# RWKV layer: the receptance products placed right behind the keys', and the weight lows of both made on GpSimd

## The reference

```python
h = rms_norm(x, mix_norm[l])
h_prev = jnp.pad(h, ((0, 0), (1, 0), (0, 0)))[:, :-1]
dx = h_prev - h
r, k, v = jnp.einsum('sbtc,scd->sbtd', h[None] + dx[None] * mu[:3, None, None, :], w_rkv)
xw, xa, xg = h + dx * mu[3], h + dx * mu[4], h + dx * mu[5]
w_log = -softplus(-(w0 + tanh(xw @ w1) @ w2)) - 0.5
decay = exp(-exp(w_log))
a = sigmoid(a0 + (xa @ a1) @ a2)
g = sigmoid(xg @ g1) @ g2
kk = (k * k_k) by head;  kk = kk * rsqrt(max(sum(kk * kk), 1e-24))
k = k * (1 + (a - 1) * k_a)
y = wkv7_scan(r, decay, k, v, -kk, kk * a)      # then a head norm, a bonus from r * k, times g, times w_o
```

## Time and profile before

| | |
|---|---|
| median of 3 runs | 2046.4 us (2046.1 to 2047.64) |
| profiled execution: time, span | 2049.06 us, 2047.7 us |
| TensorE busy | 1993.0 us, 97% |
| VectorE busy | 1512.7 us, 74% |
| ScalarE busy | 1087.5 us, 53% |
| GpSimd busy | 164.7 us, 8% |
| weight lows on VectorE | 608, mean 1241 ns |
| weight lows on GpSimd | 34, mean 2506 ns |

### The profile page before, as it was taken

The page is one execution under the profiler, slowest core; times in us unless marked ns, Lnnn a source line. Parts: engine busy times, 40 slices in busy tenths (PEclk is TensorE's granted clock), DMA queues, the critical chain, the costliest instruction groups (busy, mean ns, idle before and its releaser), DMA issues.

```text
span 2047.7 us, 33781 instructions
## 1 busy us (share of the span) xinstructions
PE 1993.0 (97%) x13456; PEld 1808.1 (88%) x13456; DVE 1512.7 (74%) x2548; ACT 1087.5 (53%) x1661; POOL 164.7 (8%) x92
## 2 busy tenths in 40 slices
PE   8999899999999999899999999999999999999999
PEld 7997789889888998689989789989999999888888
DVE  6776784877667775877757877899899996555555
ACT  6654643266555664666645765545544445555554
POOL 0000013300011000210001013232000000000000
PEclk9999998999999999999999999999999999999999
DMA  6666231156655666246666335546544446666664
GB/s 210 202 207 219 83 104 63 52 194 198 205 186 185 198 203 192 103 134 204 198 205 216 116 132 195 174 162 203 176 155 147 151 144 204 201 204 205 202 202 163
DMA packets 98173, 353.08 MB, mean 172 GB/s; under 512 B 10977, under 2 KB 12897, under 8 KB 97505
## 3 DMA queue, kind: packets, MB, share of 16 engines
q1 hardware_dynamic: 98016, 350.91, 52.9%
HBM read 349.82 MB, written 1.05 MB: 171 GB/s over the span
## 4 chain that ended last, share of the span: by engine, by line
PE 82%; DVE 11%; ACT 4%; issue 1%; POOL 1%; DMA 0%; SPq 0%; DVEq 0%; ACTq 0%
PE psum L312 17%; PE psum L314 17%; PE psum L313 17%; PE psum L326 15%; PE psum L327 7%; DVE tile_low L219 3%; PE psum L2824 2%; PE psum L950 1%; ACT tile_high L207 1%; PE psum L418 1%; PE psum L1149 1%; POOL small L1768 1%; PE psum L1029 1%; ACT hT L562 1%; ACT unread L557 0%
## 5 line engine op out<-in xcount | busy, mean ns | idle before, releaser
L219 DVE TENSOR_TENSOR tile_low<-raw_tiles,tile_high 128x1024 fp32r<-128x1024 f32 x608 | 753.0, 1241 | 354.1 <-ACT tile_high L207 353.6
L207 ACT ACTIVATE tile_high<-raw_tiles 128x1024 fp32r<-128x1024 f32 x642 | 675.0, 1053 | 400.3 <-PE psum L314 394.5
L326 PE MATMUL psum<-hT,tile_high 128*128 128x512 f32 x1408 | 463.7, 383 | 0.0
L327 PE MATMUL psum<-hT,tile_low 128*128 128x256 f32 x1408 | 383.8, 273 | 0.0
L312 PE MATMUL psum<-hT,tile_high 128*128 128x256 f32 x1152 | 324.6, 282 | 9.3 <-ACT rwkv_arena L1602 4.8
L313 PE MATMUL psum<-hT,tile_high 128*128 128x256 f32 x1152 | 317.5, 276 | 0.0
L314 PE MATMUL psum<-hT,tile_low 128*128 128x256 f32 x1152 | 317.5, 276 | 0.0
L312 PE MATMUL psum<-tile_high,hT 128*128 128x512 f32 (+1 forms) x816 | 311.4, 382 | 4.3 <-DVE tile_low L219 2.5
L313 PE MATMUL psum<-tile_low,hT 128*128 128x512 f32 (+1 forms) x816 | 307.6, 377 | 0.0
L314 PE MATMUL psum<-tile_high,hT 128*128 128x512 f32 (+1 forms) x816 | 307.6, 377 | 0.0
L326 PEld LDWEIGHTS psum<-hT,tile_high 128*128 128x128 f32 x1408 | 266.1, 189 | 37.7
(11 more groups left out here) (362 smaller groups left out, 2533.3 us busy)
## 6 DMA issues: line engine op xcount, KB each, us to landing
raw_tiles<-ffn_in_dram SPq DMA_DIRECT2D x176, 512.0 KB, 4.3
raw_tiles<-peer_u_dram SPq DMA_DIRECT2D x128, 512.0 KB, 3.4
raw_tiles<-peer_v_dram SPq DMA_DIRECT2D x128, 512.0 KB, 4.2
raw_tiles<-ffn_out_dram SPq DMA_DIRECT2D x88, 512.0 KB, 4.3
raw_tiles<-w_kv_dram SPq DMA_DIRECT2D x16, 512.0 KB, 4.2
raw_tiles<-in_gates_dram SPq DMA_DIRECT2D x16, 512.0 KB, 3.6
raw_tiles<-peer_q_dram SPq DMA_DIRECT2D x16, 512.0 KB, 4.0
raw_tiles<-w_k_dram SPq DMA_DIRECT2D x8, 512.0 KB, 4.4
```

Of the source, the lines that this page charges most:

```text
L207: scalar.activation(k.high[:, n % SLOTS, :], k.raw[:, n % RAW_SLOTS, :], ACT.Copy).then_inc(*k.tile_high_made.mark(n))
L219: vector.tensor_tensor(k.low[:, n % SLOTS, :], k.raw[:, n % RAW_SLOTS, :], k.high[:, n % SLOTS, :].bitcast(F32), ALU.subtract).then_inc(*k ...
L326: k.tensor.matmul(both_sums, high[:, c, :], both, start=(c == 0), stop=(c == KC - 1), skip_group_check=True)
L327: ins = k.tensor.matmul(both_sums[:, 0], low[:, c, :], both[:, 0], start=False, stop=(c == KC - 1), skip_group_check=True)
```

## The change

On TensorE the order behind the keys becomes: hidden products of decay and rate, sums of the squared keys, outputs of decay and rate, four receptance tiles, spread of the norms, a fifth tile, hidden products of the gate, MT, three tiles, gate outputs, MAK, values. VectorE makes mix 1 as h * (1 - mu) from ScalarE (the "own part") plus mu times the token before, and dx only behind it; then mixes 3, 4, 0, 5, the low of mix 0, and mix 2, all ahead of the norm work. It scales both token blocks. All lows of `w_k` but the first and all of `w_r` are made by GpSimd. Mixes are split in natural order and the results read from PSUM in turns. The factor 1 + (a - 1) * k_a ("rate") moves from ScalarE to VectorE. The warming products ahead of the keys are 60 in place of 68.

```diff
 def on_pool(n):
 
-    if n in SECOND_TILES:
+    if n in SECOND_TILES or FIRST["w_k"][0] < n < FIRST["w_r"][1]:
         return True
...
-def scalar_norm(k, s, xn, whole, ahead, parts=True):
+def scalar_norm(k, s, whole, share, to, ahead):
...
-    scalar.wait_ge(*k.root_made.at((s, 1)))
-    scalar.activation(xn[:, 1, :], k.x[:, 1, :], ACT.Copy, scale=k.small[:, 1:2]).then_inc(
-        *k.scaled_by_scalar.mark((s, 1)))
...
+    scalar.wait_ge(*k.decays.at("share"))
+    for half in range(2):
+        scalar.wait_ge(*k.gain_applied.at((s, 1, half)))
+        for c in range(4 * half, 4 * half + 4):
+            ins = scalar.activation(to[:, c, :], whole[:, c, :], ACT.Identity, scale=share[:, c:c + 1])
+        ins.then_inc(*k.own_part_made.mark(half))
...
 def tensor_rwkv(k):
...
+    hidden_pair()
+    key_norms()
+    lora_outputs()
+    for _ in range(4):
+        next(next_tile)
+    spread_norms()
+    next(next_tile)
+    gate_hidden("lora_g", lambda c: r["w_g1"][:, c, 0:P])
+    gate_hidden("lora_g2", lambda c: r["w_g1"][:, c, P:2 * P])
+    tensor.wait_ge(*k.scaled.at("b"))
+    for tb in range(TB):
+        tensor_scan_products(k, tb, "MT", "b_s", "a_s", k.mt_made)
+    for _ in range(3):
+        next(next_tile)
+    gate_outputs()
...
 def vector_rwkv(k):
...
+    for half in range(2):
+        mix_first(half)
+    for half in range(2):
+        mix_low(1, half)
+    vector.tensor_tensor(dx[:, :, 1:T], h[:, :, 0:T - 1], h[:, :, 1:T], ALU.subtract)
...
+    mix(3)
+    mix(4)
+    mix(0)
+    mix(5)
+    for half in range(2):
+        mix_low(0, half)
+    vector.wait_ge(*k.mix_low_made.at((1, 1)))
+    mix(2)
...
-    more = [None, (3, 0), (3, 1), (4, 0), (4, 1), (5, 0), (5, 1), None]
-    for i in range(8):
-        split_low(k, first_k + i + SLOTS)
-        if more[i]:
-            mix(*more[i])
...
 def scalar_rwkv(k):
...
-    for g in range(4):
-        evac_k(g)
+    evac_k(0)
+    evac_k(1)
+    for half in range(2):
+        mix_high(0, half)
+    evac_k(2)
+    scalar.wait_ge(*k.mix_low_made.at((0, 1)))
+    square(0)
+    evac_k(3)
+    square(1)
...
 def pool_rwkv(k):
     pool, r = k.pool, k.room["rwkv"]
     pool_norm(k, "rwkv")
+    split_low_on_pool(k, FIRST["w_r"][1])
+    pool.wait_ge(*k.pool_low_made.now())
```

More of the change, by code:

```diff
@@ L460, in vector_norm @@
             *k.mean_made.mark((s, tb)))
[L461 to L482, removed]
+    for tb in range(TB):
+        vector.wait_ge(*k.root_made.at((s, tb)))
+        vector.tensor_scalar(xn[:, tb, :], k.x[:, tb, :], k.small[:, tb:tb + 1], None, ALU.mult).then_inc(
+            *k.scaled_by_vector.mark((s, tb)))
+        if tb == 0:
+            vector.tensor_scalar(share, mu, -1.0, 1.0, ALU.mult, ALU.add).then_inc(*k.decays.mark("share"))
+    for tb in range(TB):
+        for half in range(2):
+            chunks = slice(4 * half, 4 * half + 4)
+            vector.wait_ge(*k.x_turned.at((s, tb, half)))
+            vector.tensor_tensor(whole[:, chunks, block(tb)],
+                                 result(k, ("norm", s, tb, half)).rearrange("p (c t) -> p c t", t=P),
+                                 spread(gain[:, chunks], P), ALU.mult).then_inc(*k.gain_applied.mark((s, tb, half)))
 def pool_norm(k, s):
@@ L854, in tensor_rwkv, with hidden_pair @@
     tensor_norm(k, "rwkv", r["xn"])
+    whole = r["mixed_whole"]
     def mix_ready(n):
         return lambda c: c % 4 or tensor.wait_ge(*k.mix_low_made.at((n, c // 4)))
-    other = k.room["rwkv"]["mixed"]
-    tensor_features(k, "w_k", other, mix_ready(1), fill=68)
-    def low_rank(name, n, weights):
+    tensor_features(k, "w_k", r["mixed"], mix_ready(1), fill=60)
+    decay, rate = (("lora_w", 3, slice(0, 64), r["hidden_w"]), ("lora_a", 4, slice(64, P), r["hidden_a"]))
+    def hidden_pair():
+        tensor.wait_ge(*k.loaded["w_in"].at("w_in"))
+        ps = [bank(k, name, k.lora_hidden, name) for name, _, _, _ in (decay, rate)]
+        for _, n, _, _ in (decay, rate):
+            tensor.wait_ge(*k.mixed.at((n, 1)))
+        for c in range(KC):
+            for i, (name, n, rows, _) in enumerate((decay, rate)):
+                ins = tensor.matmul(ps[i][rows, 0:T], r["w_in"][:, c, rows], whole[n][:, c, :], start=(c == 0), stop=(c == KC - 1))
+        ins.then_inc(*k.lora_done.mark("lora_w", "lora_a"))
@@ new lines, in key_norms @@
+    def key_norms():
+        ps = bank(k, "norms", k.key_norm, "largest")
+        tensor.wait_ge(*k.key_squared.at(1))
+        tensor.wait_ge(*k.loaded["masks"].at("masks"))
+        for n in range(2):
+            for quarter in range(QUARTERS):
+                c = 2 * quarter + n
+                ins = tensor.matmul(ps[rows_of(quarter), 0:T], r["norm_sel"][:, n, :], r["square"][:, c * T:(c + 1) * T],
+                                    start=(n == 0), stop=(n == 1))
+        ins.then_inc(*k.norms_summed.mark("norms"))
@@ new lines, in lora_outputs @@
+    def lora_outputs():
+        tensor.wait_ge(*k.loaded["lo"].at("lo"))
+        for name, _, _, _ in (decay, rate):
+            tensor.wait_ge(*k.lora_hidden.at(name))
+        for c in range(0, KC, 2):
+            ps = [bank(k, (name, c), k.lora_out, (name, c)) for name, _, _, _ in (decay, rate)]
+            for i in range(2):
+                for j, (_, _, rows, hidden) in enumerate((decay, rate)):
+                    ins = tensor.matmul(ps[j][:, i * T:(i + 1) * T], r["w_lo"][rows, (c + i) * P:(c + i + 1) * P], hidden,
+                                        start=True, stop=True)
+            ins.then_inc(*k.lora_used.mark(("lora_w", c), ("lora_a", c)))
@@ L869, in tensor_rwkv @@
-    pair = (("lora_w", 3, slice(0, 64)), ("lora_a", 4, slice(64, P)))
-    ps = [bank(k, name, k.lora_hidden, name) for name, _, _ in pair]
-    for name, n, _ in pair:
-        tensor.wait_ge(*k.mixed.at((n, 1)))
-    for c in range(KC):
-        for i, (name, n, rows) in enumerate(pair):
-            ins = tensor.matmul(ps[i][rows, 0:T], r["w_in"][:, c, rows], r["whole"][MIXED[n]][:, c, :], start=(c == 0),
-                                stop=(c == KC - 1))
-    ins.then_inc(*k.lora_done.mark("lora_w", "lora_a"))
@@ L1546, in mix_high @@
         scalar.wait_ge(*k.mixed.at((n, half)))
[L1547 to L1548 removed]
+        scalar.activation(to[0][:, chunks, :], whole[n][:, chunks, :], ACT.Copy).then_inc(*k.mix_high_made.mark((n, half)))
     def evac_k(g):
```

243 lines of the change are left out of this document (102 added, 141 removed).

## The result

| | before | changed |
|---|---|---|
| median (6 runs each, same chip) | 2047.0 us | 2057.7 us (2056.2 to 2060.2) |
| ratio, 95% interval | | 1.0049 (1.0036 to 1.0062) |
| profiled execution: time, span | 2049.1, 2047.7 us | 2060.2, 2058.9 us |
| lows on GpSimd | 34, mean 2506 ns | 49, mean 2581 ns |

A forecast was written before the change was run, and what follows sets the result against it. TensorE, 82% of the span, was taken as the bound. Start, stands and clock summed to +2.6 (yielding) or +10.0 us (holding); +7.5 was taken, giving 2056.6 profiled, 2054 us median; range 2035 to 2063.

The forecast's parts named there:

- Turns are taken, whole instructions: VectorE's two-SBUF-input passes, mixes included, alternate with GpSimd lows: 2046 to 2058 us, chance 0.68.
- The two rivals without collisions for the mixes: Mixes pass beside GpSimd, only tensor_tensor takes turns: 2039 us, chance 0.14; nothing collides: 2030 us, chance 0.08.
- The unlikely one on the slow side (2062): GpSimd wins the race for the second scaling and each stand keeps the clock low: +16 us, chance 0.10.
- The start: First w_k product on TensorE at 201.1, 2.6 us earlier; 202.9 if GpSimd gets in ahead of VectorE's second scaling.
- The stand of 9.1 us before the seventh tile, released by a low,: TensorE in w_k waits from 217.2 to 226.3 for w_k6's low, its high queued on ScalarE behind mix 0's.
- yielding: A waiting GpSimd instruction gets in behind each VectorE instruction: w_v +0.9 us, with clock +2.6 in all.
- Two stands "of some 4 us": TensorE waits ahead of the spread (for the reciprocal) and ahead of MT (for b), some 4 us each.
- holding: A run of VectorE instructions without waits keeps GpSimd out: w_v +7.4 us, with clock +10.0 in all.
- The wait of 1.8 us for the squares: Behind the keys, ScalarE does the first squares only behind mix 0's low: 1.8 us yielding, 0 holding.
- The list of passes that collide: VectorE passes with two SBUF inputs, mixes included, contend with GpSimd lows; with one operand in PSUM nothing happens.
- "A shift of that start is a shift of the end": Behind the first w_v product (289.71) order is unchanged and TensorE leads, so its delay reaches the kernel's end.
- GpSimd's lows in 200 to 260: Sign of turns: these lows have a mean above 2.9 us; staying at 2.38 would speak against the prediction.

The follow-up runs named there:

- experiments 1: Changed kernel with the lows of w_k1 to w_r7 back on VectorE, new product order kept: 2045.9 us, ratio 0.9990 to before.
- 6: Changed kernel with lows back on VectorE, plus two unneeded GpSimd memsets behind each high of w_k3 to w_k7: 2046.7 us, ratio 0.9986 to before.
- 7: Changed kernel with lows back on VectorE, plus one unneeded GpSimd subtract behind each high of w_k3 to w_k7: 2057.1 us, ratio 1.0039 to before.
- Experiment 2: Changed kernel with ScalarE making the highs of w_k6 and w_k7 ahead of mix 0's two: 2055.2 us, ratio 1.0034 to before.

## Why the prediction was right, and where it was off

**Turns are taken, whole instructions** (0.68 of the chances): shown, by experiments 1, 6 and 7. The two rivals without collisions for the mixes fall: 32 mixes take 19.1 us, not 13.0, and the time is 19 and 28 us above theirs. The unlikely one on the slow side (2062) had its first part right, GpSimd's win at the second scaling: 2.83 for 0.75.

**The start** was given as 201.1, or 202.9 if that race is lost. It was lost: 203.4, or 202.8 without the 0.6 us of this trace.

**The stand of 9.1 us before the seventh tile, released by a low,** with ScalarE's queue as the cause, came as worked out for yielding: 9.9. Experiment 2 shows the queue's part.

**Two stands "of some 4 us" by the reciprocal and by b:** 3.2 and 5.0.

**What was mis-sized:**
- *The choice between yielding and holding.* I took +7.5, near the +10.0 of holding. The stage measured +6.7, but in the keys' first lows by yielding, which was priced at +0.9 and 1.7 of clock, 2.6 in all (2049 us). That the number was close is in part luck. Of the missing 4.1 us, 2.7 are w_k6's low: it asked at 223.93 and ended at 229.47, held out 3.2 us in the midst of a kernel that else yields, and TensorE went on at 229.0 (without the 0.6) where 226.3 was worked out. Another 1.0 is the clock: behind the long stand 26 products ran at half clock in 5.7 us, in place of 2.9 at the 0.113 each of the tiles ahead, so 2.7 lost and not 1.7. The rest, 0.4, is as much as my own sum was short: from b at 272 its terms add to 291.0, not 290.6. The wait of 1.8 us for the squares, priced under yielding, did not come. The lost scaling race hardly counts, since TensorE waited for w_k6 anyway.
- *The list of passes that collide.* I counted passes with two SBUF inputs. The rate on VectorE (tensor_scalar, one tensor input) took 6.70 in place of 2.66 beside two lows, and a copy of 128x16 took 2.18 in place of 0.17. Both lie on the way to b.
- *"A shift of that start is a shift of the end".* From inside the stage `w_v` is 6.7 us late, the program 10.6 (medians; 11.2 of span less 0.6). The values took 34.8 us in place of 33.1 at a granted clock of 0.90 in place of 0.95, and by the last turning product of y (398.14 against 389.48) the delay is 8.1. The other 2.5 lie behind, 1.2 of them at the start of the next feed-forward stage; I did not follow them.
- *GpSimd's lows in 200 to 260* have a mean of 2.85, not above 2.9: GpSimd lost less, VectorE as much as said.

What was costed at nothing stayed so: reading PSUM in turns (ScalarE's evacuations of 128x512 take 0.60 before and after), and the memsets (the first inverse step waits for no GpSimd). The later loads were not tried by themselves.

The change joins a gain and a loss, here by the ratios: the order of the products (-2.0 us as first tried, with an interval from -3.9 to -0.2; -13.7 once the two queues are paced to it and two lows are on GpSimd where they cost little) and the lows on GpSimd (+9.2 in the old order, +12.1 in the new).

## What to carry to other kernels

Work moved to GpSimd is not free because GpSimd is idle: each 2.4 us read of SBUF there took up to 2.1 us from VectorE, more than the 1.17 us for which VectorE does the same low. Move it only under stretches in which VectorE reads PSUM or idles, and look at VectorE's durations, not its busy share, which was 100% of 26.2 us while 8 of them were waiting. And when a product order changes, set the splits in each queue by when TensorE wants them: here the reordering alone gave 2.0 us, and this pacing nearly all of the 11.7 more.
